# Gate loads of the branch stage issued by SyncE between the weight blocks instead of by GpSimd

## The reference

```python
gates = jax.nn.sigmoid(gate_pre).reshape(Bn, S, N_BRANCH, D_MODEL)
y_a = o_a @ w_branch[:A_WIDTH]
y_b = o_b @ w_branch[A_WIDTH:A_WIDTH + B_WIDTH]
y_c = o_c @ w_branch[A_WIDTH + B_WIDTH:]
mixed = gates[:, :, 0] * y_a + gates[:, :, 1] * y_b + gates[:, :, 2] * y_c
x = x + mixed @ w_out
```

## Time and profile before

| | us |
|---|---|
| median of 3 runs | 3476.6 |
| their range | 3472.49 to 3476.61 |
| the profiled execution, whole | 3469.55 |
| its span, first to last instruction | 3467.9 |
| TensorE busy in the span | 3187.6 |

### The profile page before, as it was taken

How to read it: one execution, slowest core, us unless ns; L and a number is a source line. 1 busy time by engine, 2 the same in 40 slices (tenths; PEclk the granted TensorE clock), 3 DMA queues, 4 the chain that set the end, 5 groups by cost and what they waited for, 6 DMA issues and landing times.

```text
span 3467.9 us, 45725 instructions
## 1 busy us (share of the span) xinstructions
PE 3187.6 (92%) x17652; PEld 2913.2 (84%) x17652; DVE 1571.5 (45%) x3225; ACT 1170.1 (34%) x2480; POOL 508.1 (15%) x872
## 2 busy tenths in 40 slices
PE   6789999898988999999977999989989899999998
PEld 6788888787877899999877888887878878999997
DVE  5345245754455333443463452457544553434433
ACT  4244334465532221111143343344655222212110
POOL 0111322221143000000001113222211420000000
PEclk9899999999999999999989999999999999999999
DMA  3424343333266122211033344434332752112211
GB/s 125 145 95 135 119 141 119 122 113 113 71 191 200 37 61 73 73 52 56 31 123 112 104 127 129 142 112 128 113 100 70 207 177 61 61 49 73 72 39 65
DMA packets 273368, 358.63 MB, mean 103 GB/s; under 512 B 27440, under 2 KB 209904, under 8 KB 273176
## 3 DMA queue, kind: packets, MB, share of 16 engines
q1 hardware_dynamic: 214520, 182.59, 17.3%
q0 software_dynamic: 58656, 173.50, 15.9%
HBM read 264.42 MB, written 91.59 MB: 103 GB/s over the span
## 4 chain that ended last, share of the span: by engine, by line
PE 35%; DVE 6%; ACT 4%; issue 2%; DMA 2%; POOL 1%; SPq 0%; ACTq 0%; POOLq 0%; DVEq 0%
PE ps L1842 11%; PE ps L1768 7%; PE ps L1770 7%; PE ps L1769 7%; ACT arena L1184 1%; DVE wl L1367 1%; DMA stage<-gate_t 1%; PE ps L1911 1%; PE ps L1959 1%; PE ps L1899 1%; DVE stage L1405 0%; DVE stage L1402 0%; ACT wh L1090 0%; DVE head_s L1396 0%; DVE c_s L1661 0%
## 5 line engine op out<-in xcount | busy, mean ns | idle before, releaser
L1768 PE MATMUL ps<-wh,xh 128*128 128x384 f32 (+1 forms) x1440 | 543.4, 377 | 12.1 <-DVE wl L1367 6.4
L1769 PE MATMUL ps<-wl,xh 128*128 128x384 f32 (+1 forms) x1440 | 524.0, 364 | 0.0
L1770 PE MATMUL ps<-wh,xl 128*128 128x384 f32 (+1 forms) x1440 | 523.8, 364 | 0.0
L1768 PE MATMUL ps<-xh,wh 128*128 128x384 f32 (+1 forms) x1184 | 410.5, 347 | 19.5 <-DVE stage L1433 8.7
L1367 DVE TENSOR_TENSOR wl<-wraw,wh 128x1024 fp32r<-128x1024 f32 (+2 forms) x210 | 232.4, 1111 | 398.7 <-ACT wh L1090 398.2
L1770 PE MATMUL ps<-xh,wl 128*128 128x384 f32 (+1 forms) x1184 | 398.0, 336 | 0.0
L1769 PE MATMUL ps<-xl,wh 128*128 128x384 f32 (+1 forms) x1184 | 397.9, 336 | 0.0
L1842 PE MATMUL ps<-xh,wh 128*128 128x384 f32 x1408 | 361.4, 337 | 20.1 <-DVE arena L1755 15.3
L1842 PE MATMUL ps<-xl,wh 128*128 128x384 f32 x1408 | 358.8, 335 | 0.0
L1842 PE MATMUL ps<-xh,wl 128*128 128x384 f32 x1408 | 358.5, 335 | 0.0
L1768 PEld LDWEIGHTS ps<-wh,xh 128*128 128x128 f32 x1440 | 279.3, 194 | 42.8 <-DVE wl L1367 6.7
(11 more groups left out here) (223 smaller groups left out, 5002.2 us busy)
## 6 DMA issues: line engine op xcount, KB each, us to landing
wraw<-in_w_in SPq DMA_DIRECT2D x96, 512.0 KB, 3.7
wraw<-in_w_ffn_in SPq DMA_DIRECT2D x88, 512.0 KB, 3.8
wraw<-in_w_in SPq DMA_DIRECT2D x72, 384.0 KB, 3.4
wraw<-in_w_ffn_out SPq DMA_DIRECT2D x44, 512.0 KB, 3.2
qkv_a<-stage POOLq DMA_DIRECT2D x108, 192.0 KB, 2.2
gate_t<-stage POOLq DMA_DIRECT2D x96, 192.0 KB, 2.2
stage<-gate_t POOLq DMA_DIRECT2D x78, 192.0 KB, 4.6
mix_t<-stage POOLq DMA_DIRECT2D x52, 192.0 KB, 4.3
```

Of the source, the lines that this page charges most:

```text
L1768: pe.matmul(out, ah, bh, start=first, stop=False)
L1769: pe.matmul(out, ah, bl, start=False, stop=False)
L1770: return pe.matmul(out, al, bh, start=False, stop=last)
```

## The change

GpSimd no longer loads gates. SyncE does, in between its weight blocks. Ahead of weight block n it issues all gates up to two past the number of jobs that are done when block n-3 is split; the waits for a free buffer are the same ones, now on SyncE.

```diff
+                    def load_gates(first, end):
+                        for i in range(first, end):
+                            _, b, d, q = MIX_LIST[i]
+                            if i == 0:
+                                for r in range(SLOTS):
+                                    sp.wait_ge(stored[r], 16 * ((len(STAGED) - 1 + SLOTS - r) // SLOTS))
+                            if i - GSLOTS >= MIX_LAST:
+                                sp.wait_ge(r_lo, i - GSLOTS - MIX_LAST + 1)
+                            elif i >= GSLOTS:
+                                sp.wait_ge(mix_stored[i % GSLOTS], 16 * (i // GSLOTS))
+                            elif i == GSLOTS - 1:
+                                sp.wait_ge(b_dec, len(B_UNITS))
+                            sp.dma_start(gated[i % GSLOTS], gate_t[b, d * P:(d + 1) * P, HALVES[q]]
+                                         ).then_inc(gate_in[i % GSLOTS], 16)
+
+                    JOBS_AT = {n: len([x for x in STEPS[:STEPS.index(step) + 1] if x in MIXES])
+                               for step, subs in SPLITS.items() for c, n in subs}
+                    first_gate = 0
...
                             n = FIRST_SUB[c] + j
+                            last_gate = min(JOBS_AT.get(n - RAW, 0) + GSLOTS - 3, len(MIXES))
+                            if last_gate > GSLOTS - 3:
+                                load_gates(first_gate, last_gate)
+                                first_gate = max(first_gate, last_gate)
                             if n >= RAW:
                                 sp.wait_ge(w_lo, n - RAW + 1)
...
+                    load_gates(first_gate, len(MIXES))
...
-                        if m == len(STAGED) - 1:
-                            wait_stage(m)
-                            for i in range(GSLOTS - 2):
-                                load_gate(i)
...
-                        if i + GSLOTS - 2 < len(MIXES):
-                            load_gate(i + GSLOTS - 2)
```

More of the change, by code:

```diff
@@ L837, in wait_mix_stored @@
                         pool.wait_ge(mix_stored[i % GSLOTS], 16 * (i // GSLOTS + 1))
[L839 to L849, removed]
                     def load_part(j):
```

## The result

Over 20 runs of each the changed kernel takes 3481.61 us (3472.95 to 3489.73), the kernel before 3475.3 (3470.45 to 3484.45). The ratio is 1.0018 [1.0011, 1.0025]: the change costs about 6 us, at the edge of what the prediction called the same. 3480 was forecast.

What follows compares the result with a forecast made beforehand. TensorE was taken as the bound, its 22.5 us of idle time in the branch stage limiting any gain. The terms -2.8 + 7.2 - 1.4 = +3.0 us gave 3480 us on the median, range 3465 to 3493.

Steps and rivals of the forecast that it cites:

- The bound: Whole kernel: a change of the gate loads can't win more than TensorE's idle time in the branch stage, 22.5 us.
- b = 1: Branch stage, jobs 16 to 31: groups of four jobs get shorter, winning 2.8 us over both layers.
- The group of four: Jobs 16 to 31: split, block, gate and multiplication take 9.9 us per four jobs, against 10.1 and 10.4 before.
- The prediction's test: Jobs 16 to 31: VectorE's gate waits come at jobs 19, 23, 27 and 31, hardly at others.
- block ahead of the gate: Rival, branch stage: blocks keep each layer's landing, 6.3 and 8.3 us, delaying gates; sum +9.4 us, 3486; chance 0.34.
- The second loop of the prediction: Jobs 16 to 31: the loop over five buffers takes 13.0 us for five jobs, 10.4 for four, no gain.
- b = 2: Branch stage, jobs 32 to 47: gates 39 and 43 come late behind split and block, losing 7.2 us over both layers.
- Partial sums: Branch stage: part loads issue without gate issue or waits ahead, winning 0.7 us in each layer, 1.4 in all.
- Start of the stage and b = 0: Branch stage before job 16: gates 15 and 17 come perhaps 1 to 3 us later, covered by filled banks, costing nothing.
- The sum: Whole kernel: -2.8 + 7.2 - 1.4 = +3.0 us, forecast as 3480 us; chance 0.25.
- Full DMA engines: Rival, jobs 16 to 31: moving gates only changes the order, no gain there; sum +5.8 us, 3482; chance 0.17.
- The short queue: Rival, branch stage: block and gate land sooner on SyncE's queue, groups take 8.6 us; sum -13 us, 3463; chance 0.24.

Runs made afterwards that it cites:

- e8: e4 with the accumulating stores of b = 1 made plain, leaving the products of b = 0 out of the sum; 3457.57 us, ratio 0.9941.
- e3: The changed kernel, but from job 16 on gate 4k+3 is issued directly ahead of the weight block, not behind it; 3469.36 us, ratio 0.998.
- e4: The changed kernel with SyncE issuing gates up to four past the jobs done, where it stopped at two; 3461.38 us, ratio 0.9958.
- e2: The kernel before, but SyncE loads gates 35 to 47 only and GpSimd still gates 0 to 34; 3481.24 us, ratio 1.0013.
- e1: The changed kernel, but SyncE loads only gates 0 to 34 and GpSimd gates 35 to 47 as before; 3477.31 us, ratio 1.0008.
- e6: The kernel before, all gates on GpSimd, but gate i+4 instead of gate i+3 issued in job i; 3502.84 us, ratio 1.0078.
- e7: The kernel before with the accumulating stores of b = 1 made plain, leaving out the products of b = 0; 3460.42 us, ratio 0.9955.

## Why the prediction came out right, step by step

**The bound.** It held. The most that any kernel won is 21 us of the stage (e8, which leaves work out), against the 22.5 us of idle time that the prediction read as the limit.

**b = 1: forecast -2.8 us, measured -0.7, which one trace can't tell from nothing.** The group of four was forecast at 9.9 us; it takes 9.95 in the first layer (39.81 / 4) and 10.4 in the second. Its steps can be read one by one. From job 4k to the issue of the block it is 1.9 us in every group, as forecast. From there to the multiplication of job 4k+3 it is 5.6 to 7.0 us in the first layer, 6.4 on average, and 6.0 to 8.8 in the second, 6.9 on average, where 7.2 was assumed. And from job 4k+3 to 4k+4 it is 1.7 and 1.6 us on average instead of 0.6. The last is the term that was mis-sized, "job 4k+4 directly after it, since its gate came with the same group". Two groups of the first layer, jobs 27 and 28, 31 and 32, and SyncE's queue ahead of the first two:

```profile
1045.83 0.56 DVE L1440 TENSOR_TENSOR stage<-ps,stage 128x384 f32<-128x384 f32 x1 [4.10 <-DMA stage<-gate_t]
1047.38 0.56 DVE L1440 TENSOR_TENSOR stage<-ps,stage 128x384 f32<-128x384 f32 x1 [0.99 <-DMA stage<-gate_t]
...
1056.20 0.56 DVE L1440 TENSOR_TENSOR stage<-ps,stage 128x384 f32<-128x384 f32 x1 [4.71 <-DMA stage<-gate_t]
1057.92 0.56 DVE L1440 TENSOR_TENSOR stage<-ps,stage 128x384 f32<-128x384 f32 x1 [1.17 <-DMA stage<-gate_t]
```

```profile
1039.59 0.39 SPq L789 DMA_DIRECT2D wraw<-in_w_out  x1
1040.03 1.07 SPq L770 DMA_DIRECT2D stage<-gate_t  x2
```

Gates 27 and 28 are issued within 1.07 us of each other, and still the second is waited for 0.99 us more.

The prediction's test was whether the waits come at jobs 19, 23, 27 and 31 and hardly at others. The long ones do: 3.58, 4.10 and 4.71 us at 19, 27 and 31 in the first layer (the 4.80 at 23 are put down to TensorE), 2.78, 5.35, 5.38 and 5.26 in the second. At jobs 16, 17, 20, 22, 24, 28 and 32 they are 0.5 to 2.7. So the block ahead of the gate is there as forecast. What the sum left out is that before had the same waits at the same jobs (4.13 us at 27, 3.27 at 31). GpSimd issues gate 27 0.4 us ahead of the block there, in the other queue, and job 27 starts 8.04 us behind job 24, at 1045.07; in after the gate is issued 0.4 us behind the block, and it is 8.10:

```profile
1038.45 0.86 POOL L848 DMA_DIRECT2D stage<-gate_t  x1
1038.88 0.37 SPq L766 DMA_DIRECT2D wraw<-in_w_out  x1
```

In this group the other queue saved the gate nothing. What helps is to stand ahead of the block in its own queue: in e3, where gate 27 is issued half a microsecond ahead of it there, job 27 starts 5.1 us behind job 24. Job 28, whose gate is behind the block there, pays for it, and the group takes 10.4 us all the same.

The second loop of the prediction, over the five buffers, was forecast at 10.4 us for four jobs, close to the 9.95 and 10.4 of the group, so b = 1 of after can't tell the two apart by its length. In e4, where gates 4k+3 and 4k+4 no longer wait for the split, the loop gives 0.6 + 1.0 + 5.8 + 0.4 + 4.3 = 12.1 us for five jobs with that kernel's gates (4.3 us to landing); sixteen take 38.7 by that and took 37.3. With plain stores (4.0 us to landing in e8, gates 4.0) it is 10.0 us, under the 10.3 that TensorE needs for five, and TensorE is busy throughout. Both fit the loop; since the landings are taken from the same traces, and the 1.0 is an estimate, they don't prove it.

**b = 2: forecast +7.2 for the gates and, with the partial sums, +5.8; measured +1.6 and +2.6, so +4.2.** The mechanism is the forecast one, shown by e2, e3 and e4. The waits at 39 and 43 are there, 1.82 and 3.24 us, 2.02 and 3.26 in the second layer; from the multiplication behind which the split stands to the end of that split it is 1069.27 to 1073.18, 3.9 us where 4.1 was forecast. e2 shows that the loss needs nothing of b = 1, and e3 that the block ahead of the gate is enough to cause it. Two sizes were off. Block and gate take 4.7 us for gate 39 (1073.34 to 1078.05) and 6.1 for gate 43, where 6.3 was forecast for both. And the steps began with gate 39, but gate 35 stands behind a block too and is waited for 2.83 and 3.05 us. Together VectorE waits 7.9 and 8.3 us for gates ahead of job 45, more than the 3.6 of the sum.

**Partial sums: forecast -1.4 for the span; this term was wrong and hid the other.** They had cost more than I counted (12.8 us, where the earlier trace rows has 10.4 for one tile alone), and all of it went. Before w_out VectorE waits 6.7 and 6.1 us for parts in before, the longest just ahead of job 45, and not at all in after. The first of these rows is before, the other two are e4:

```profile
1089.52 0.56 DVE L1440 TENSOR_TENSOR arena<-arena 128x384 f32<-128x384 f32 x1 [3.12 <-DMA arena<-mix_t]
```

```profile
1061.75 0.56 DVE L1447 TENSOR_TENSOR arena<-arena 128x384 f32<-128x384 f32 x1 [1.81 <-DMA arena<-mix_t]
...
1084.05 0.56 DVE L1447 TENSOR_TENSOR arena<-arena 128x384 f32<-128x384 f32 x1 [1.72 <-DMA arena<-mix_t]
```

The lighter GpSimd is at most a part of it: in e4 GpSimd is as free of gates as in after, and without gate waits behind job 33 the part waits ahead of job 45 are back at 4.3 and 3.8 us. It seems that the gate waits give the parts their time, though no run tests this alone. One stall took the place of the other, 16.2 us of gate waits for 12.8 of part waits, +3.4, and the stage shows +4.2. What GpSimd's freedom alone is worth is at most 6.7 - 4.3 and 6.1 - 3.8, 4.7 us in the two layers, which no run separates from the larger lead; e1, where GpSimd has the late gates, has 6.0 and 5.8.

**Start of the stage and b = 0: forecast nothing.** Jobs 12 to 16 are 0.2 and 0.4 us shorter, and TensorE is busy all 22.00 us from 1012 to 1034. It held.

**The sum.** +3.0 was forecast, the stage gives +2.9, 2.7 at equal clock. This close a sum owes much to luck. Errors cancel in it, since -2.8 and +5.8 were -0.7 and +4.2 (and 12 to 16 -0.6), and b = 1 alone differs by 1 to 2 us from trace to trace. The 3480 was counted from the median of three runs, 3476.6, 1.3 us above that of the twenty. The last 3 us of the measured 6.3 have no term in the forecast and go with the granted clock.

**w_out.** The delay of the stage is passed on whole: TensorE starts w_out 2.4 us later, and ScalarE meets the norm of the next stage at 1142.80 instead of 1140.35. That gate 47 costs nothing also held: from 1096 to 1106 TensorE is busy 9.64 of 10 us although job 47 waits 2.66 for its gate (before, 10.00 from 1094 to 1104).

**The rivals.** Full DMA engines would give +5.8 and lie inside the measured interval, but e4 rules them out: with a share of 1.04 the sixteen jobs of b = 1 took 3 us less. The Trainium skill, "DMA: Bandwidth & Descriptors", "Issuing engines are not separate DMA queues", lets another issuer save sequencer time only. For the change as made this agrees: e1 wins nothing. But e6 against e4 shows what the rule leaves out, the waits that an engine's order brings with it: the two kernels have the same transfers and a lead of four gates both, and their stages differ by 43 us. The short queue is refuted (b = 1 would have taken 34.4 us). The block ahead of the gate is the right mechanism. In b = 2 it stands as in the sum, at 4.7 to 6.1 us from block to job instead of 6.3; in b = 1 it is there too, but before had paid it already, so the +3.6 of that rival (groups of 9.7 and 11.7 us) didn't come: they are 9.95 and 10.4.

## What to carry to other kernels

When loads move to another engine, look first at what each of them will wait for and stand behind there. The issue time saved is small; here a 512 KB block directly ahead of a 192 KB gate cost 4 us of the stage, one swap of the two gave that back, and the same engine with a lead of four gains 12 us, as the loads that came late then wait only for their buffers. An engine that issues stores must not wait in front of them. Stalls in series on one engine cover each other, so before counting a removed wait as won, list which other load is nearly late behind it. And where executions differ by more than the effect, compare the stage by its own times in the trace, and run the same code twice before believing 1 or 2 us of it. Here the sums of the stage (+2.9, -12.1 and -21.1 us for after, e4 and e8) fit the differences at equal clock (+2.7, -12.6 and -21.2) better than they fit the medians. They don't for e6 (+30.7 against +17.0), where the clock fell within the stage.

## What the hardware showed that I had not expected

- A DMA share of 1.00 to 1.04 isn't a full machine: with it, 16 jobs took 40.35, 39.8 or 37.3 us, at 222, 227 and 242 GB/s.
- A block of 512 KB directly ahead in SyncE's queue delays a gate by less than the block's own landing time and the gate's together: 4.7 to 6.1 us for both in b = 2, where blocks take 5.0 us to land and gates 5.3.
- A gate issued 0.4 us ahead of a block from the other queue lands no sooner than one issued 0.4 us behind it in the block's own queue: the job starts 8.04 and 8.10 us behind the one that triggers both (job 27, before and after). Issued 0.5 us ahead of it in the block's own queue (e3), it is 5.1 us.
- Accumulating stores are dear to those around them: with plain ones (e7, 1017 to 1057 us) the stores land in 5.0 instead of 5.8 us and the gates in 4.6 instead of 5.2, and b = 1 is 11 us shorter in the two layers together.
- The granted clock of the same kernel varies between executions (0.969 to 0.974 for before), and 0.001 of it goes with 2.9 us, as much as the stage's whole change. In e6, where TensorE waits most in the stage, it fell to 0.91 to 0.93 there.
